# Spreading the key scores and the top-k over the query groups, with PSUM operands for the matches, in a hybrid decoder layer

## The reference

```
xn = rms_norm(h); q,k,v for 8 softmax heads and 8 stick-breaking heads = xn @ w_in
h += concat(rms_norm(o_m), rms_norm(o_s)) @ w_out
x2 = rms_norm(h)
qk = x2 @ w_query                       # 8 heads x 2 halves x 128
s1, s2 = qk[..., :128] @ sub_keys[0].T, qk[..., 128:] @ sub_keys[1].T
v1,i1 = top_k(s1, 16); v2,i2 = top_k(s2, 16)
top_s, top_pos = top_k(v1[:, None] + v2[None, :], 16)     # 16 of 256 pairs
expert = i1[a] * 128 + i2[b]; gates = softmax(top_s)
h += sum over the 8 x 16 experts of gates * gelu(x2 . u[expert]) * v[expert]
h += sigmoid(rms_norm(h) @ w_gate) * (p @ w_ple)
```

## Time and profile before

| | |
|---|---|
| median of the runs | 1023.03 us |
| profiled execution, its own time | 1021.96 us |
| its span (first to last instruction) | 1020.2 us |
| TensorE busy | 993.6 us, 97% |
| VectorE busy | 670.8 us, 66% |
| ScalarE busy | 493.8 us, 48% |
| GpSimd busy | 346.9 us, 34% |
| mean granted TensorE clock | 0.997 |

### The profile page before, as it was taken

How to read it: one execution, slowest core, us unless ns; L and a number is a source line. 1 busy time by engine, 2 the same in 40 slices (tenths; PEclk the granted TensorE clock), 3 DMA queues, 4 the chain that set the end, 5 groups by cost and what they waited for, 6 DMA issues and landing times.

```text
span 1020.2 us, 18777 instructions
## 1 busy us (share of the span) xinstructions
PE 993.6 (97%) x6490; PEld 904.2 (89%) x6490; DVE 670.8 (66%) x1289; ACT 493.8 (48%) x693; POOL 346.9 (34%) x145
## 2 busy tenths in 40 slices
PE   8999989999998999999999999999999999999998
PEld 5987879999998999999999999888888888878877
DVE  5647663299999423787788777566655555677663
ACT  6476543544444464333333333555555555656643
POOL 0002020389989877666666665000000000020000
PEclk9999989999999999999999999999999999999999
DMA  8662421054454554334333433555567777545511
GB/s 302 225 229 83 171 91 75 22 186 165 165 184 145 185 173 165 137 144 144 134 134 143 144 137 130 186 192 199 185 218 237 247 237 241 195 177 188 201 64 42
DMA packets 43798, 168.87 MB, mean 166 GB/s; under 512 B 5075, under 2 KB 6524, under 8 KB 42492
## 3 DMA queue, kind: packets, MB, share of 16 engines
q1 hardware_dynamic: 43392, 168.46, 47.0%
q10 hardware_dynamic: 380, 0.07, 0.0%
HBM read 167.45 MB, written 1.06 MB: 165 GB/s over the span
## 4 chain that ended last, share of the span: by engine, by line
PE 79%; POOL 7%; issue 6%; DVE 5%; DMA 1%; ACT 1%; POOLq 0%; SPq 0%; DVEq 0%; ACTq 0%
PE bank L1342 11%; PE bank L1344 11%; PE bank L1345 11%; PE bank L1062 10%; PE bank L1063 10%; PE bank L1064 10%; POOL t_lo L1029 7%; PE bank L1302 6%; PE bank L1087 2%; PE bank L1089 2%; PE bank L1088 2%; DVE w_lo L621 1%; PE bank L1385 1%; PE bank L1387 1%; PE bank L1386 1%
## 5 line engine op out<-in xcount | busy, mean ns | idle before, releaser
L1029 POOL TENSOR_TENSOR t_lo<-t_raw,t_hi 128x1024 fp32r<-128x1024 f32 x130 | 328.0, 2529 | 169.9 <-ACT t_hi L495 169.6
L1062 PE MATMUL bank<-xt_hi,t_hi 128*128 128x256 f32 x1024 | 296.3, 289 | 7.4 <-POOL t_lo L1029 6.7
L495 ACT ACTIVATE t_hi<-t_raw 128x1024 fp32r<-128x1024 f32 x256 | 270.8, 1058 | 62.7 <-DMA t_raw<-v_chunks 56.8
L1064 PE MATMUL bank<-xt_hi,t_lo 128*128 128x256 f32 x1024 | 289.9, 283 | 0.0
L1063 PE MATMUL bank<-xt_lo,t_hi 128*128 128x256 f32 x1024 | 289.8, 283 | 0.0
L774 DVE TENSOR_TENSOR t_lo<-t_raw,t_hi 128x1024 fp32r<-128x1024 f32 x126 | 155.5, 1234 | 96.7 <-ACT t_hi L495 96.5
L1062 PEld LDWEIGHTS bank<-xt_hi,t_hi 128*128 128x128 f32 x1024 | 196.3, 192 | 9.3 <-ACT slots L513 7.1
L1342 PE MATMUL bank<-t_hi,g_hi 128*128 128x512 f32 x512 | 199.7, 390 | 3.4 <-DVE g_lo L950 2.2
L1344 PE MATMUL bank<-t_lo,g_hi 128*128 128x512 f32 x512 | 199.4, 390 | 0.0
L1345 PE MATMUL bank<-t_hi,g_lo 128*128 128x512 f32 x512 | 199.4, 389 | 0.0
L1063 PEld LDWEIGHTS bank<-xt_lo,t_hi 128*128 128x128 f32 x1024 | 196.6, 192 | 0.0
(11 more groups left out here) (200 smaller groups left out, 1268.3 us busy)
## 6 DMA issues: line engine op xcount, KB each, us to landing
t_raw<-u_chunks SPq DMA_DIRECT2D x128, 512.0 KB, 3.2
t_raw<-v_chunks SPq DMA_DIRECT2D x128, 512.0 KB, 3.3
w_raw<-w_in SPq DMA_DIRECT2D x4, 2048.0 KB, 8.5
w_raw<-w_query SPq DMA_DIRECT2D x4, 2048.0 KB, 7.8
w_raw<-w_in SPq DMA_DIRECT2D x8, 512.0 KB, 9.1
w_raw<-w_out SPq DMA_DIRECT2D x2, 2048.0 KB, 7.6
wg_raw<-w_gate SPq DMA_DIRECT2D x8, 512.0 KB, 4.9
h<-x SPq DMA_DIRECT2D x2, 512.0 KB, 4.4
```

What stands on the lines that cost most here:

```text
L495: nc.scalar.activation(t_hi[:, q % RING, :], t_raw[:, q % RING, :], ACT.Copy).then_inc(t_hi_ready, 1)
L1029: nc.gpsimd.tensor_tensor(t_lo[:, q, :], t_raw[:, q, :], t_hi[:, q, :].bitcast(f32), ALU.subtract).then_inc(t_lo_pool, 1)
L1062: mm(dst, ah, bh, start=(c == 0), stop=False)
L1064: ins = mm(dst, al, bh, start=False, stop=(c == n - 1))
```

## The change

- TensorE computes the two score units of query group n - 1 right behind query group n, and those of group 3 behind group 3 too (`key_scores`). ScalarE copies them out in between (`scores_out`).
- VectorE waits for each pair of units by itself and runs `halves` for both token tiles, group by group. `scores`, `top_v`, `top_i` and `rest` move to other places in SBUF.
- `top_f` (the numbers as floats) and `pos_m` (four of the small tiles of `positions`) move to PSUM, and the compare reads its numbers from `lanes` in PSUM instead of from `iota` in SBUF. `top_f` has one tile for both token tiles; one of the tiles, `pos_n`, stays in SBUF, so that no instruction has two inputs in PSUM.
- The ones of slots 64 to 127 are written by ScalarE, in 16 activations of 128 x 1024 (Relu with scale 0 and bias 1), one in each of the steps 48 to 63, behind the step's Gelu. VectorE's memsets go.
- EXP_AT becomes 44 and PICKS_AT 48.

```diff
-        scores = tile("scores", [P, TT, PG, N_KEYS], BIG + 4 * 20480)
+        scores = tile("scores", [P, TT, PG, N_KEYS], UP + 4 * 4096)
...
+        top_f = bank[3][:, P:P + PG * TOPK].rearrange("p (g k) -> p g k", g=PG)
+        pos_m = bank[1][:, :].rearrange("p (n k) -> p n k", n=4)
... ScalarE
+            def scores_out(n):
+                for tt in range(TT):
+                    u = TT * n + tt
+                    act.wait_ge(s_done, u + 1)
+                    nc.scalar.copy(scores[:, tt, 4 * n:4 * n + 4, :]..., bank[SCORE_BANKS[u]][:, :])
             query_part(0)
             split_group(10)
             query_part(1)
+            scores_out(0)
             split_group(11)
             query_part(2)
+            scores_out(1)
             query_part(3)
             for n in range(LEAD):
                 table_hi(n, 1)
-            for u in range(8): ... copy of unit u
+            scores_out(2)
+            scores_out(3)
...
-            u_steps(EXP_AT + RING, FIRST)
+            act.wait_ge(hit_used, 2 * TT)
+            ones_end = EXP_AT + RING + (N_KEYS - FIRST) // ONES
+            with act.Fori((EXP_AT + RING) // RING, ones_end // RING) as i:
+                for q in range(RING):
+                    table_hi(q + LEAD, i + 1 + (q + LEAD) // RING)
+                    u_gelu(q, i)
+                    late = slots[:, ... ONES slots ..., :]
+                    nc.scalar.activation(late, iota broadcast, ACT.Relu, scale=0.0, bias=1.0
+                                         ).then_inc(ones_ready, 1)
... VectorE
-            dve.wait_ge(s_out, 8)
-                link(nc.vector.tensor_copy(top_f[:, tt, :, :], top_i[:, tt, :, :]))
+                link(nc.vector.tensor_copy(top_f, top_i[:, tt, :, :]))
-                number_of = iota[:, 0:TOPK]... ; number = top_f[:, tt, :, :]...
+                number_of = lanes[:, 0:TOPK]... ; number = top_f...
-            for tt in range(TT):
-                for g in range(0, PG, 2):
-                    halves(tt, g)
+            for n in range(4):
+                for tt in range(TT):
+                    dve.wait_ge(s_out, TT * n + tt + 1)
+                    for g in (4 * n, 4 * n + 2):
+                        halves(tt, g)
+            dve.wait_ge(lanes_ready, 1)
+            for tt in range(TT):
                 pairs_of(tt) ... best_of, positions, picked
-            for n in range(FIRST, N_KEYS, 8):
-                ins = nc.vector.memset(slots[:, n:n + 8, :], 1.0)
...
                 if nth == 1:
                     dve.wait_ge(gelu_done, FIRST)
+                    dve.wait_ge(ones_ready, (N_KEYS - FIRST) // ONES)
... TensorE
+            def key_scores(n):
+                if n == 0:
+                    pe.wait_ge(sk_loaded, 16)
+                pe.wait_ge(query_ready, 2 * (n + 1))
+                ... the two units of group n, as before
             for n in range(4):
                 ...
                 columns_group(QUERY0 + n, 2 * (n % 2))
+                if n:
+                    key_scores(n - 1)
+            key_scores(3)
```

More of the change, by code:

```diff
@@ L47 @@
 FIRST = 64
-EXP_AT = 52
-PICKS_AT = 56
+EXP_AT = 44
+PICKS_AT = 48
+ONES = 4
 BLOCKS = ((0, 1, 16), (1, 3, 8), (4, 4, 4), (8, 8, 1))
@@ L110, in layer_program @@
         slots = tile("slots", [P, N_KEYS, SEQ], BIG)
-        scores = tile("scores", [P, TT, PG, N_KEYS], BIG + 4 * 20480)
+        scores = tile("scores", [P, TT, PG, N_KEYS], UP + 4 * 4096)
         o = UP
[L114 to L117, removed]
+        top_v = tile("top_v", [P, TT, PG, TOPK], ZONE + 4 * 6144)
+        top_i = tile("top_i", [P, TT, PG, TOPK], ZONE + 4 * 6656, u32)
+        rest = tile("rest", [P, 2, 256], ZONE + 4 * 5120)
         cand = tile("cand", [P, PH, PAIRS], o); o += 4 * PH * PAIRS
@@ L121, in layer_program @@
         pos_f = tile("pos_f", [P, 3, PH * TOPK], o); o += 4 * 384
-        pos_m = tile("pos_m", [P, 4, PH * TOPK], o); o += 4 * 512
+        pos_n = tile("pos_n", [P, PH * TOPK], o); o += 4 * 128
         pos_ab = tile("pos_ab", [P, 2, PH * TOPK], o); o += 4 * 256
-        assert o <= BIG + 4 * P * SEQ
+        assert o <= UP + 4 * 4096
         wg_raw = tile("wg_raw", [P, DC, D], BIG)
@@ L213, in layer_program @@
         t_hi_ready, t_lo_ready, t_lo_pool = sem("t_hi_ready"), sem("t_lo_ready"), sem("t_lo_pool")
-        lanes_ready, late_used = sem("lanes_ready"), sem("late_used")
+        lanes_ready, ones_ready, late_used = sem("lanes_ready"), sem("ones_ready"), sem("late_used")
         table_row = sem("table_row")
@@ L485, in query_part @@
                                    bank[2 * (n % 2) + q][:, :]).then_inc(query_ready, 1)
+            def scores_out(n):
+                for tt in range(TT):
+                    u = TT * n + tt
+                    act.wait_ge(s_done, u + 1)
+                    nc.scalar.copy(scores[:, tt, 4 * n:4 * n + 4, :].rearrange("p a b -> p (a b)"),
+                                   bank[SCORE_BANKS[u]][:, :]).then_inc(s_out, 1)
             query_part(0)
@@ L529, in _ @@
                 u_gelu(q, EXP_AT // RING)
-            u_steps(EXP_AT + RING, FIRST)
+            act.wait_ge(hit_used, 2 * TT)
[4 more added lines that the diff above has]
+                    u_gelu(q, i)
+                    late = slots[:, bass.ds((i - (EXP_AT + RING) // RING) * (RING * ONES) + (FIRST + ONES * q), ONES), :]
+                    nc.scalar.activation(late.rearrange("p n (a b) -> p (n a) b", b=P),
+                                         iota.unsqueeze(1).to_broadcast([P, 2 * ONES, P]), ACT.Relu, scale=0.0,
+                                         bias=1.0).then_inc(ones_ready, 1)
+            if ones_end < FIRST:
+                u_steps(ones_end, FIRST)
             def late_step(q, i):
@@ L837, in positions @@
                 nc.vector.scalar_tensor_tensor(out=m0, in0=a, scalar=16.0, in1=m2, op0=ALU.mult, op1=ALU.min)
-                link(nc.vector.scalar_tensor_tensor(out=m1, in0=a, scalar=48.0, in1=m3, op0=ALU.add, op1=ALU.min))
-                link(nc.vector.tensor_tensor(m2, m0, m1, ALU.min))
+                link(nc.vector.scalar_tensor_tensor(out=pos_n[:, :], in0=a, scalar=48.0, in1=m3, op0=ALU.add,
+                                                    op1=ALU.min))
+                link(nc.vector.tensor_tensor(m2, m0, pos_n[:, :], ALU.min))
                 link(nc.vector.tensor_tensor(b, c, m2, ALU.subtract))
@@ L845, in picked @@
             def picked(tt, q):
-                number_of = iota[:, 0:TOPK].unsqueeze(1).unsqueeze(1).to_broadcast([P, PH, TOPK, TOPK])
+                number_of = lanes[:, 0:TOPK].unsqueeze(1).unsqueeze(1).to_broadcast([P, PH, TOPK, TOPK])
                 place = pos_ab[:, q, :].rearrange("p (a b) -> p a b", a=PH).unsqueeze(3).to_broadcast(
                     [P, PH, TOPK, TOPK])
-                number = top_f[:, tt, :, :].rearrange("p (h two) k -> p h two k", two=2)[:, :, q, :].unsqueeze(
-                    2).to_broadcast([P, PH, TOPK, TOPK])
+                number = top_f.rearrange("p (h two) k -> p h two k", two=2)[:, :, q, :].unsqueeze(2).to_broadcast(
+                    [P, PH, TOPK, TOPK])
                 def summed():
@@ L882, in _ @@
                         step()
-            for n in range(FIRST, N_KEYS, 8):
-                ins = nc.vector.memset(slots[:, n:n + 8, :], 1.0)
-            link(ins)
             gates_of_picks()
@@ L889, in _ @@
                 nc.vector.tensor_copy(pick_t[:, q, :], half(q, 0)).then_inc(pick_t_out, 1)
-            dve.wait_ge(lanes_ready, 1)
             def one_hots(k, s):
@@ L1249, in _ @@
             transposes(2, TT)
+            def key_scores(n):
[3 more added lines that the diff above has]
+                for tt in range(TT):
+                    t = slice(P * tt, P * (tt + 1))
+                    for q in range(4):
+                        g = 4 * n + q
+                        ins = mm(bank[SCORE_BANKS[TT * n + tt]][:, P * q:P * (q + 1)], query[:, g, t],
+                                 sk[:, g % 2, :], start=True, stop=True)
+                    ins.then_inc(s_done, 1)
             for n in range(4):
```

## The result

The changed kernel takes 1015.09 us, median of four runs (1014.62 to 1015.72), against 1023.61 us for the kernel before in the same comparison; the ratio is 0.9922, with a 95% interval of 0.9903 to 0.9940. The forecast was 1014.9 us. The profiled execution took 1014.62 us with a span of 1012.9 us.

A forecast was written before the change was run, and what follows sets the result against it. TensorE, busy 97% of the span, was taken to bound the kernel, with eight u-step stalls on GpSimd's `t_lo`. Terms -9.3 + 0.9 + 0.3 = -8.1 us gave 1014.9 us against the median, range 1012.3 to 1018.8.

The forecast's parts named there:

- The cause of the stalls: U steps: VectorE's compare and multiply with two SBUF inputs take turns with GpSimd's `t_lo`, so TensorE waits eight times.
- The size, 9.3 us: U steps, 247.25 to 327.74 us: all eight TensorE stalls go, 9.3 us by distance of starts; bounds 0 to 9.3.
- The price of the new order, 0.9 us and 0.3 us: Start of u steps: late `t_lo` costs 0.9 us from the third step; three more matmul-kind changes cost 0.3 us.
- Exp at 44: U steps: the detour of two table loads and Exp cost TensorE 0.2 us and only moves, costing that again.
- The earlier top-k and the moved memsets, nothing: VectorE: starting top-k at 178.3 us and losing 8 memsets of 1.76 us bring no time by themselves.
- Rival 1: U steps: only part of the stalls goes, as the multiply still holds up `t_lo`; 1017.1 to 1018.7 us, chance 0.11.
- Rival 3: Steps 48 to 63: fills push ScalarE's turn beyond TensorE's 2.88 us; 1047 us at 3.6 us fills; chance 0.05 + 0.04.
- The sum: Whole kernel: stalls gone, late start and matmul-kind changes together, -9.3 + 0.9 + 0.3 = -8.1 us.

The follow-up runs named there:

- psum_only: The kernel before with only the operands of the matches and of `positions` moved to PSUM, old order kept: 1013.76 us, ratio 0.9918.
- matches_sbuf: The whole change with `top_f` and the compare's numbers back in SBUF, `pos_m` still in PSUM: 1024.34 us, ratio 1.0018 against the kernel before.
- multiply_sbuf: The whole change with only `top_f` back in SBUF, so the multiply has two SBUF inputs and the compare one: 1017.24 us, ratio 0.9940.
- early_hi: The whole change with ScalarE's first two `t_hi` ahead of its copy of the last query group: 1013.87 us, ratio 0.9914.
- ones_vector: The whole change with the ones written by VectorE's 8 memsets again, behind the picks, and no ScalarE fills: 1015.28 us, ratio 0.9931.
- fill_8: The whole change with ScalarE's fills of 8 slots (128x2048) in 8 steps, same total: 1014.58 us, ratio 0.9919.
- fill_16: The whole change with ScalarE's fills of 16 slots (128x4096) in 4 steps, same total: 1022.32 us, ratio 0.9993.
- wp_pieces: The whole change with GpSimd's one 128x2048 `wp_lo` split into eight pieces of 128x256: 1010.72 us, ratio 0.9874.

## Why the prediction was right

**The cause of the stalls.** Right, and shown from both sides: one part alone brings all (psum_only), all but the compare's and the multiply's operands brings none (matches_sbuf), and with the multiply's operand back in SBUF a quarter of the cost or less is there (multiply_sbuf). Two VectorE inputs in SBUF and a GpSimd instruction that reads SBUF take turns (4.37 us instead of 2.29); one input moved to PSUM ends it, though the output stays in SBUF.

**The size, 9.3 us.** Right: 9.5 us between the third u step and step 65, with the 0.2 of the Exp detour. It was right because it was taken from the distance of starts and not from the listed idle time of 7.3.

**The price of the new order, 0.9 us and 0.3 us.** The 0.9 is right: the first u step is 1.2 us late (1.15 worked out), the third 1.0 (0.9), and up to step 65 the change takes 0.92 us more than psum_only. early_hi takes the first wait away, and shows that it was this `t_hi`. The 0.3 for three more changes between kinds of matmul is wrong: early_hi, which has them all, reaches the first u step in 41.41 us, the old order in 41.42. I had read 0.08 us a change from one pair of rows; in the sum of the stretch it isn't there.

**Exp at 44.** Off by a little: I said its 0.2 us would move along; in the change TensorE lost under 0.1 us there.

**The earlier top-k and the moved memsets, nothing.** Right: psum_only (1013.76 us) has neither and ones_vector (1015.28) lacks only the second, and neither is slower than the change beyond the scatter. Their cover held: the weight split of group 3 was ready at 177.1 us, and the group began at about 181.5.

**Rival 1.** Its price was about right: I gave 1017.1 to 1018.7 for a multiply that still holds up `t_lo`, and multiply_sbuf, which makes it so, took 1017.24.

**Rival 3.** The mechanism exists, but further off than I put it. I had 0.3 to 0.4 us of ScalarE's idle time left and a decision at a fill of 1.45 us. Left were 0.60 us. From fill_8 (3.02 with a fill of 1.92) and fill_16 (4.72 with 3.62), a turn without idle time is the fill plus 1.10 us. As an estimate it binds at 2.88 - 1.10 = 1.78 us, and by 8.1/16 more, for 16 fills, the gain is gone at 2.29. No run had 16 fills of that length.

**What the sum left out, and luck.** Up to step 65 the change wins 8.53 us, 9.45 less 0.92, and the medians differ by 8.5. The sum said 8.1. The spans of the two profiled executions differ by 7.3 only, because of the clock behind the `g_lo` wait, about which the prediction said nothing. Nine traces have this wait, with 2.6 to 3.9 us between starts. Six show a stretch at 1.2 GHz behind it (the change, psum_only, matches_sbuf, multiply_sbuf, early_hi, fill_16) and three don't (before, ones_vector, fill_8). The one kept trace of the kernel before happens to be one of the three. That the time came within 0.2 us of the forecast (1015.09 against 1014.9) is in part luck: the gain was 0.4 us larger than the sum, and the kernel before was 0.6 us slower in this comparison (1023.61) than in the runs that I reckoned from (1023.03).

## What to carry to other kernels

When VectorE and GpSimd work side by side and GpSimd feeds the bound engine, look for VectorE instructions with two SBUF inputs whose rows are much longer than those of their free kin, and put one operand into a free PSUM bank. Or cut the longer of the two instructions into pieces: what a partner waits is the length of one instruction, and a supply that is n microseconds ahead can swallow the first n. The pieces together may take longer than the whole did (9.63 us against 5.09 here), so cut where the sum has room. Measure a stall by the distance of starts, and ask of each rearrangement beside such a fix what it brings alone; here it cost 0.9 us.

## What the runs showed of the hardware

- TensorE's wait of 2.2 us near 900 us was followed, in the change, by a stretch at 1.2 GHz, and in the kernel before, after a wait of the same length, it wasn't. The length alone doesn't decide it: with 2.59 us between starts (the change) and 2.76 (psum_only) the clock fell, with 2.62 (before), 2.74 (ones_vector) and 2.78 (fill_8) it didn't. With the waits of up to 1.67 us in the u steps (fill_16) it stayed at 1.00 in all traces. So such a wait can cost 1.7 times its length: in the change 2.4 us of stall and 1.6 us at the lower clock. wp_pieces, which took away the wait, is 4.4 us faster by the medians.
- Two inputs of VectorE in SBUF: a 128x2048 `hit` took up to 4.50 us beside GpSimd's `t_lo`; with one of them in PSUM, 2.29 us, and `t_lo` 2.41 us.
- Relu after a Gelu table load, and copies after it, brought no further table load; 16 fills of 128x1024 took 1.05 us each.
- Memsets of VectorE (1.76 us each) and reduces (2.29 us) didn't touch GpSimd's 2.41 us (2.40 to 2.42 in ones_vector); a reduce has one SBUF input and a memset none.
